# A hybrid GLA, RWKV-7 and SSD layer with 32 experts on one core: the opening's loads and the place of eight small products are moved

## The chip, the cores and the metric

The kernel runs on one core of a Trainium2 chip. The time is the device time of one execution in microseconds (us), from which the median of several runs is taken. The matrix engine is called PE (TensorE), the vector engine DVE (VectorE), the activation engine ACT (ScalarE), the general engine POOL (GpSimd), and SP is the engine that issues the DMAs (SyncE).

## The reference

One layer over 256 latent tokens (x) and 256 context tokens (ctx), model width 1024:

```
mod_l = split(silu(c) @ w_ada + b_ada, 6); mod_c = the same for c_ctx
hl = modulate(rmsnorm(x, norm1_g), mod_l[0], mod_l[1])      # h * (1 + scale) + shift
hc = modulate(rmsnorm(ctx, norm1_g), mod_c[0], mod_c[1])
u  = h @ w_in      -> q, k, v, og, gates (GLA) | RWKV-7 | z, x, B, C, dt (SSD)
x, B, C of the SSD group: silu(depthwise convolution of width 4 over the tokens + bias)
GLA:  o_t = sum_s q_t k_s exp(cum_t - cum_s) v_s, both directions
RWKV-7 and SSD: chunked scans in both directions, the context first
xl = x + mod_l[2] * (concat(gla, rwkv, ssd) @ w_out)
hl = modulate(rmsnorm(xl, norm2_g), mod_l[3], mod_l[4])
moe: router, top 4 of 32 experts; act = glu * sigmoid(1.702 glu) * (lin + 1) ; y += gate * (act @ w_down + b)
out = rmsnorm(xl + mod_l[5] * y, final_norm_g)
```

All weights of the 32 experts are read once: 12 MB each.

## The kernel before, in words

The program is written out by hand for each engine; the order in the code is the order in which an engine runs. Engines meet at semaphores. Results of PE lie in banks of PSUM; a table (`round_table`) gives every result a name and a pair of banks, and a result may only be written (`R.claim`) when the one before it in the same pair has been read out (`R.drained`). B, xs0 and z0 use pair 0 in turn; C, xs1 and z1 pair 1; the nine levels l0 to l8 pair 2; gs, gc, Bt and gS pair 3.

**The opening.** Eight slices k of 128 features each need `ada[k]` (the modulation weights, 1 MB) and `opened[k]` (576 KB: the transposed tokens and a part of the weights); `tokens` (4 DMAs of 512 KB) serve only the root mean squares. ACT squares the four token tiles and takes the root, DVE the reciprocal, and PE spreads the reciprocals over the partitions (`roots_spread`, 4 products). A row of modulation (`modulation_row`, 32 products), its copy by ACT and two products (`modulation_columns`) give the scales of a slice; DVE and ACT scale the slice, and PE projects it. In between PE does `stay_busy(n)`: n products of the identity that nobody reads, in the numbers WARM. A product of this kernel is in fp32 and stands as two matmuls in the trace, so stay_busy(26) is x52.

**The levels.** GLA's causal products are built in nine levels. POOL writes the arguments of a level (4 instructions, L788 to L791), ACT takes their exponent (`level_exp`, L945), DVE multiplies them with keys and queries (`level_keys(i)`, L1424, which feeds level i+1), PE multiplies (`level(i, 0)` and `level(i, 1)`, 4 small products each), and DVE takes the result out (`level_out(i)`; L1249, L1251, L1254). Level i may start when `level_out(i-1)` has read the pair of banks. POOL's arguments of level i+2 wait for `level_keys(i)`. Between the levels PE projects; a half projection (early, late) is 4 products of 128x512.

**Convolutions.** A convolution starts on ACT (`conv_start`, L899) with the centre tap, goes on with `convolve` on DVE (L1345, 12 instructions for 512 tokens), and ends with silu on ACT (`conv_end`). `convolve` also frees the banks of its projection. `multiplied(n)` (L1292, L1290) are DVE's products of later modulation weights, one for each `ada` DMA, between the rest; it frees the slot for a later DMA.

**The experts.** SP loads 12 MB for each of 32 experts into a ring of slots that PE frees.

Of the kernel before, what the change touches and what calls it, by code (L numbers as in the profile page):

```python
# [169 lines left out]
WARM = (10, 4, 26, 7)  # L170
# [21 lines left out]
def round_table():  # L192
    t = []
    for m in range(KD):
        t += [(f"row{m}", 4, 1), (f"col{m}", 2, 1 if m == KD - 1 else 0)]
        if m == 0:
            t.append(("roots", 2, 0))
    t += [("ll", 3, 2), ("gq", 1, 1), ("gv", 0, 1), ("dtp", 4, 1), ("gz", 2, 1), ("og", 1, 1), ("dt", 3, 1), ("gk", 2, 1), ("B", 0, 1),
          ("gvt", 2, 1), ("gs", 3, 1), ("gc", 3, 1)]
    t += [("C", 1, 1), ("ms1", 4, 1), ("mt1", 4, 1), ("xs0", 0, 1), ("xs1", 1, 1)]  # L200
    t += [(f"l{i}", 2, 1) for i in range(9)]
    t += [("z0", 0, 1), ("z1", 1, 1), ("Bt", 3, 1), ("gS", 3, 1), ("rk", 1, 1), ("sc", 0, 1), ("cc", 3, 1), ("xst0", 2, 1), ("go", 3, 1), ("xst1", 2, 1)]
    t += [("ms2", 4, 1), ("mt2", 4, 1), ("rz0", 1, 1), ("cs", 3, 1), ("rz1", 1, 1), ("rr", 0, 1), ("gn", 3, 1), ("st", 1, 1), ("sg", 1, 1), ("rkn", 1, 1)]
# [71 lines left out]
def hybrid_block(nc, a):  # L275

    with ExitStack() as ctx:
# [202 lines left out]
        ident_in = sem("ident_in")  # L480
# [10 lines left out]
        silu_c, root_ready, rms_ready, mod_ready = named("silu_c root_ready rms_ready mod_ready")  # L491
# [18 lines left out]
        f_sq, out_ready, out_done, half_up, bias_up = named("f_sq out_ready out_done half_up bias_up")  # L510
# [76 lines left out]
        for s, width, kind, n in loads:  # L587
            base[s] += 1
            place[kind, n] = (s, base[s])
            if kind == "opened":  # L590
                continue
            before[kind, n] = sorted({h for h in holder[s:s + width] if h})
            given[s] += 1
            free_at[kind, n] = (s, given[s])
            for q in range(s, s + width):
                holder[q] = (s, given[s])
# [33 lines left out]
        def _(sp):  # L630
# [11 lines left out]
            sp.dma_start(Cb(C_ID), a["consts"][:, 0:P]).then_inc(ident_in, 16)  # L642
            for k in range(KD):
                if k == 1:
                    for i in range(4):
                        sp.dma_start(xtok[:, i, :], a["tokens"][i]).then_inc(x_in[i], 16)
                load_ada(k)
                sp.dma_start(opened[:, k, :], a["opened"][k]).then_inc(slot_full[ADA_SLOTS[k]], 16)
                if k in (3, 6):
                    load_ada(8 + k // 4)  # L650
# [204 lines left out]
        def _(act):  # L855
# [16 lines left out]
            def row_copied(m):  # L872

                R.arrived(act, f"row{m}")
                R.drained(f"row{m}", act.copy(modrow[:, 64 * m:64 * m + 64], pair(f"row{m}", 512)[:, 64 * m:64 * m + 64]))

            row_copied(0)
# [6 lines left out]

            for k in range(KD):
                act.wait_ge(mod_ready, k + 1)
                if k == 0:
                    act.wait_ge(rms_ready, 2)
# [63 lines left out]

            level_exp(0)
            level_exp(1)
            conv_start("B")
# [302 lines left out]
        def _(dve):  # L1258
# [18 lines left out]

            def multiplied(n):

                sl, nth = place["ada", n]  # L1280
                if n == 16:
                    R.arrived(dve, "ms1")
                dve.wait_ge(slot_full[sl], 16 * nth)
                by_row = csil[:, n % 8, 0:1]
                flat = mod_products.rearrange("p m c -> p (m c)")
                if n % 8:
                    last, count = free_at["ada", n - 1]
                    dve.wait_ge(slot_free[last], count)
# [14 lines left out]
            for k in range(KD):  # L1303
                s, nth = place["opened", k]
                dve.wait_ge(slot_full[s], 16 * nth)
                if k:
                    step(dve.tensor_tensor(raw[:, k, :], raw[:, k, :], pair("roots")[:, 0:NT], ALU.mult))
# [10 lines left out]
                if k == 0:  # L1318
                    dve.wait_ge(root_ready, 1)
                    dve.reciprocal(small[:, 12:16], small[:, 8:12]).then_inc(rms_ready, 1)  # L1320
                    R.arrived(dve, "roots")
                    dve.tensor_tensor(raw[:, 0, :], raw[:, 0, :], pair("roots")[:, 0:NT], ALU.mult).then_inc(rms_ready, 1)
                    dve.wait_ge(rms_ready, 2)
# [103 lines left out]
            R.emptied(dve, "gq")  # L1427
            level_keys(0)
            level_keys(1)
            level_out(dve, 0)  # L1430
            convolve(0, "B")
# [417 lines left out]
            def activate(n, up_done, by_halves=False):  # L1849
# [3 lines left out]
                for half in range(2):  # L1853
# [4 lines left out]
                    if by_halves:  # L1858
                        of_half = lambda x: PS[:, half, 256 * x:256 * x + 256].rearrange("p (q k) -> p q k", k=2)
                        if half == 0:  # L1860
                            dve.wait_ge(half_up, 1)
                        else:
                            up_done()
# [104 lines left out]
        def _(pe):  # L1968
# [48 lines left out]
            def roots_spread():  # L2017

                R.claim(pe, "roots")
                pe.wait_ge(rms_ready, 1)  # L2020
# [108 lines left out]

            modulation_row(0)  # L2130
# [3 lines left out]
            roots_spread()  # L2134
            stay_busy(WARM[3])
# [45 lines left out]
            project_in("C", 1)  # L2181
            level(1, 0)
            project_in("xs0", 0, early)
            level(1, 1)
            project_in("xs0", 0, late)
            level(2, 0)
            project_in("xs0", 1, early)
            level(2, 1)
            project_in("xs0", 1, late)
            level(3, 0)  # L2190
            project_in("xs1", 0, early)
            level(3, 1)
            project_in("xs1", 0, late)
            modulation_sums(1)
            level(4, 0)
            project_in("xs1", 1, early)
            level(4, 1)
            project_in("xs1", 1, late)
            sums_by_feature(1)
            def running_sums(q):  # L2200
# [619 lines left out]
            def up_by_halves(n, at, hidden, between):  # L2820
# [13 lines left out]
                for j in range(4):  # L2834
                    r, used = at(j)
                    pe.wait_ge(ring_full[r], used * 16 + 16)
                    for k, hf in ((2 * j, 0), (2 * j + 1, 0), (2 * j, 1), (2 * j + 1, 1)) if j == 3 else ((2 * j, 0), (2 * j, 1), (2 * j + 1, 0), (2 * j + 1, 1)):
                        ins = part(k, hf)
                        if (k, hf) == (7, 0):
                            ins.then_inc(half_up, 1)  # L2840
# [3 lines left out]
                    if 1 <= j < 3:  # L2844
                        x = j - 1
                        pe.wait_ge(te_ready, n + 1)
                        if x:
                            pe.wait_ge(bias_up, 1)
# [4 lines left out]
                        if x == 0:  # L2853
                            ins.then_inc(bias_up, 1)
# [224 lines left out]
```

## Time and profile before

| what | value |
|---|---|
| median of 3 runs | 1322.54 us (1314.92, 1322.54, 1323.43) |
| the profiled execution | 1317.88 us |
| its span, first to last instruction | 1316.1 us |
| PE busy | 1246.7 us, 95% |
| DVE, ACT, POOL busy | 401.6, 261.2, 50.4 us |
| DMA, mean over the span | 347 GB/s |

The profile is of one execution, 1.8 us of which lie outside the span. Times in the views count from the span's start. Up to some 200 us the engines share the work of the projections; from there to 370 us run the scans, and from 410 us the experts.

### The profile page before, as it was taken

How to read it: one execution, taken by the hardware profiler on the slowest of the kernel's cores; microseconds unless marked ns; L12 is line 12 of the kernel's file. 1: busy time of each engine (PE TensorE's matmuls, PEld its weight loads, DVE VectorE, ACT ScalarE, POOL GpSimd, SP SyncE). 2: the span in 40 equal slices, each digit the busy share in tenths (PEclk: the TensorE clock that was granted, in tenths of full speed). 3: DMA queues.
4: the chain of work that ended last, by engine and by line, in shares of the span. 5: the costliest groups of instructions: out<-in, count | busy, mean ns of one | idle time of the engine just before them, and what ended most of it. 6: DMA issues, size and time to landing. Idle time of an engine off the chain costs nothing.

```text
span 1316.1 us, 22353 instructions
## 1 busy us (share of the span) xinstructions
PE 1246.7 (95%) x9546; PEld 589.9 (45%) x9546; DVE 401.6 (31%) x906; ACT 261.2 (20%) x601; POOL 50.4 (4%) x89
## 2 busy tenths in 40 slices
PE   8999999889899999999999999999999999999997
PEld 6464656678874333333333333333333333333333
DVE  1457766654442211121111221211221111121112
ACT  3142218543332110111100110100111010011001
POOL 0022100311100000000000000000000000000000
PEclk9999999999999999999999999999999999999999
DMA  9953520243479999999999999999999999999994
GB/s 377 397 193 128 220 108 1 90 144 96 125 279 384 425 426 427 428 429 429 426 429 429 430 427 427 429 430 429 427 428 427 428 428 427 428 427 428 426 427 200
DMA packets 41407, 456.13 MB, mean 347 GB/s; under 512 B 4624, under 2 KB 4880, under 8 KB 12912
## 3 DMA queue, kind: packets, MB, share of 16 engines
q1 hardware_dynamic: 41328, 454.96, 83.1%
q8 instruction: 64, 1.05, 0.3%
q14 instruction: 15, 0.12, 0.0%
HBM read 453.89 MB, written 1.05 MB: 346 GB/s over the span
## 4 chain that ended last, share of the span: by engine, by line
PE 84%; DVE 6%; DMA 5%; issue 2%; ACT 1%; POOL 0%; SPq 0%; DVEq 0%
PE PS L1972 80%; DMA arena<-in_moe_w_gu 3%; DMA arena<-in_moe_b_down 2%; PE PS L2869 2%; DVE arena L1865 1%; DVE arena L1868 1%; DVE arena L1871 1%; PE PS L2860 1%; DVE arena L1345 1%; PE PS L1986 1%; DVE arena L1864 1%; DMA arena<-in_opened 1%; PE PS L2464 0%; POOL arena L790 0%; DVE arena L1965 0%
## 5 line engine op out<-in xcount | busy, mean ns | idle before, releaser
L1972 PE MATMUL PS<-arena 128*64 128x512 f32 (+12 forms) x9174 | 1200.3, 402 | 26.0 <-issue 10.4
L1972 PEld LDWEIGHTS PS<-arena 64*64 64x64 f32 (+6 forms) x9174 | 549.4, 144 | 627.4 <-issue 563.6
L1864 DVE TENSOR_SCALAR arena<-PS 128x256 f32<-128x256 f32 x64 | 38.6, 604 | 505.8 <-PE PS L1972 505.8
L1178 ACT ACTIVATE arena<-arena 128x256 f32<-128x256 f32 x64 | 26.7, 417 | 477.2 <-DVE arena L1864 477.2
L1893 DVE TENSOR_TENSOR arena<-PS,arena 128x512 f32<-128x512 f32 x32 | 22.1, 692 | 214.5 <-PE PS L1972 214.5
L1188 ACT COPY arena<-PS 128x256 f32<-128x256 f32 x32 | 11.9, 373 | 281.0 <-PE PS L2860 281.0
L2869 PE MATMUL PS<-arena 128*128 128x128 f32 x128 | 26.3, 287 | 32.6 <-DVE arena L1871 32.6
L1169 ACT ACTIVATE arena<-PS,arena 128x128 f32<-128x128 f32 x128 | 48.2, 457 | 35.7 <-PE PS L1972 35.7
L2869 PEld LDWEIGHTS PS<-arena 128*128 128x128 f32 x128 | 14.3, 141 | 59.9 <-DVE arena L1871 43.0
L1630 DVE COPY arena<-PS 128x384 f32<-128x384 f32 (+2 forms) x48 | 23.4, 490 | 54.1 <-PE PS L1972 53.7
L1865 DVE TENSOR_SCALAR arena<-PS 128x256 f32<-128x256 f32 x64 | 39.1, 612 | 0.0
L1345 DVE SCALAR_TENSOR_TENSOR arena<-PS,arena 128x255 f32<-128x255 f32 (+5 forms) x68 | 32.6, 481 | 20.2 <-ACT arena L980 14.0
L1292 DVE SCALAR_TENSOR_TENSOR arena<-arena 128x2048 f32<-128x2048 f32 x14 | 33.1, 2363 | 7.0 <-DMA arena<-in_ada 6.9
L1091 ACT COPY arena<-PS 128x384 f32<-128x384 f32 (+2 forms) x48 | 20.5, 427 | 58.7 <-PE PS L1972 58.6
L1868 DVE SCALAR_TENSOR_TENSOR arena<-arena 128x256 f32<-128x256 f32 x64 | 27.2, 425 | 3.9
L1871 DVE TENSOR_TENSOR arena<-arena 128x256 f32<-128x256 f32 x64 | 27.2, 426 | 2.3
L1183 ACT COPY arena<-PS 128x256 f32<-128x256 f32 x64 | 23.7, 370 | 4.3 <-PE PS L2869 4.3
L1840 DVE TENSOR_SCALAR arena<-arena 128x128 f32<-128x128 f32 x64 | 19.1, 342 | 0.0
L1986 PE MATMUL PS<-arena 128*128 128x128 f32 x94 | 14.5, 323 | 3.3 <-DMA arena<-in_consts 3.3
L2860 PEld LDWEIGHTS PS<-arena 128*128 128x128 f32 x64 | 6.5, 141 | 24.3 <-issue 24.3
L1827 DVE TENSOR_SCALAR arena<-arena 128x64 f32<-128x64 f32 x64 | 15.7, 308 | 2.0 <-PE PS L1972 1.9
L1986 PEld LDWEIGHTS PS<-arena 128*128 128x128 f32 x94 | 13.7, 233 | 3.5 <-DMA arena<-in_consts 3.3
(263 smaller groups left out, 395.0 us busy)
## 6 DMA issues: line engine op xcount, KB each, us to landing
arena<-in_moe_w_gu SPq DMA_DIRECT2D x124, 2048.0 KB, 22.5
arena<-in_moe_w_down SPq DMA_DIRECT2D x63, 2048.0 KB, 24.3
arena<-in_ada SPq DMA_DIRECT2D x24, 1024.0 KB, 7.4
arena<-in_w_in SPq DMA_DIRECT2D x4, 2048.0 KB, 9.6
arena<-in_moe_w_gu SPq DMA_DIRECT2D x32, 256.0 KB, 3.0
arena<-in_opened SPq DMA_DIRECT2D x8, 576.0 KB, 19.0
arena<-in_tokens SPq DMA_DIRECT2D x4, 512.0 KB, 8.5
arena<-in_w_out SPq DMA_DIRECT2D x2, 1024.0 KB, 5.8
```

The costliest lines, as they stand in the source:

```text
L1169: ins = act.activation(hg[:, buffer, k, :], PS[:, bank, P * j:P * j + P], ACT.Identity, bias=scales[:, 1, k:k + 1], scale=scales[:, 0, k:k ...
L1178: act.activation(sgm[:, 256 * half:256 * half + 256], glu[:, 256 * half:256 * half + 256], ACT.Sigmoid, scale=ALPHA).then_inc(sig_ready, 1)
L1183: act.copy(actT[:, 2 * half:2 * half + 2].rearrange("p a b c -> p (a b c)"), src).then_inc(actT_ready, 1)
L1292: ins = dve.scalar_tensor_tensor(out=flat, in0=slots[sl], scalar=by_row, in1=flat, op0=ALU.mult, op1=ALU.add)
L1345: ins = dve.scalar_tensor_tensor(out=d_, in0=s_, scalar=wgt, in1=d_, op0=ALU.mult, op1=ALU.add)
L1864: dve.tensor_scalar(by_rest(glu), of_half(0), LIMIT, None, ALU.min).then_inc(glu_ready, 1)
L1865: dve.tensor_scalar(by_rest(lin), of_half(1), LIMIT, -LIMIT, ALU.min, ALU.max).then_inc(moe_vec, 1)
L1868: dve.scalar_tensor_tensor(out=lin[:, cols], in0=lin[:, cols], scalar=1.0, in1=glu[:, cols], op0=ALU.add, op1=ALU.mult).then_inc(moe_vec, 1)
L1871: dve.tensor_tensor(act_[:, cols], lin[:, cols], sgm[:, cols], ALU.mult).then_inc(act_ready, 1)
L1972: ins = pe.matmul(out, lhsT, rhs, start=start, stop=stop, skip_group_check=skip)
L1986: pe.matmul(PS[:, 0, 0:P], ident, ident, start=True, stop=True)
L2869: ins = pe.transpose(dst[:, c * P:c * P + P], act_[:, (2 * half + c) * P:(2 * half + c + 1) * P], ident)
```

## The change

SP issues the four token DMAs ahead of `ada[0]` and `opened[0]`. `opened[0]` has a semaphore of its own. ACT takes the squares and the root ahead of copying the first modulation row; DVE's reciprocal stands ahead of the loop over the slices; PE's `roots_spread` stands ahead of the first row. WARM becomes (30, 3, 6): 30 filling products, then the roots, the row, 3, the columns, 6, and the loop. Before it was 10, the row, 4, the columns, 26, the roots, 7.

In the middle ACT starts B's convolution ahead of the exponents of levels 0 and 1, and DVE convolves B ahead of `level_keys(0)`; `level_out(0)` stands ahead of `level_keys(1)`. Every half of levels 1 to 4 stands one half projection later on PE. In the experts two semaphores are made one (`last_up`), in the last expert alone; its waits come to the same.

```diff
-WARM = (10, 4, 26, 7)
+WARM = (30, 3, 6)
...
 def round_table():
-    t = []
+    t = [("roots", 2, 0)]
     for m in range(KD):
         t += [(f"row{m}", 4, 1), (f"col{m}", 2, 1 if m == KD - 1 else 0)]
-        if m == 0:
-            t.append(("roots", 2, 0))
...
             sp.dma_start(Cb(C_ID), a["consts"][:, 0:P]).then_inc(ident_in, 16)
+            for i in range(4):
+                sp.dma_start(xtok[:, i, :], a["tokens"][i]).then_inc(x_in[i], 16)
             for k in range(KD):
-                if k == 1:
-                    for i in range(4):
-                        sp.dma_start(xtok[:, i, :], a["tokens"][i]).then_inc(x_in[i], 16)
                 load_ada(k)
-                sp.dma_start(opened[:, k, :], a["opened"][k]).then_inc(slot_full[ADA_SLOTS[k]], 16)
+                sp.dma_start(opened[:, k, :], a["opened"][k]).then_inc(slot_full[ADA_SLOTS[k]] if k else opened_in, 16)
...
             act.activation(small[:, 60:61], small[:, 59:60], ACT.Sqrt)
-            row_copied(0)
             for i in range(4):
...
             act.activation(small[:, 8:12], small[:, 0:4], ACT.Sqrt, scale=1.0 / D, bias=small[:, 59:60]).then_inc(root_ready, 1)
+            row_copied(0)
...
+            conv_start("B")
             level_exp(0)
             level_exp(1)
-            conv_start("B")
             level_exp(2)
...
+            dve.wait_ge(root_ready, 1)
+            dve.reciprocal(small[:, 12:16], small[:, 8:12]).then_inc(inverse_ready, 1)
...
             R.emptied(dve, "gq")
+            convolve(0, "B")
             level_keys(0)
+            level_out(dve, 0)
             level_keys(1)
-            level_out(dve, 0)
-            convolve(0, "B")
             multiplied(14)
...
+            roots_spread()
             modulation_row(0)
             stay_busy(WARM[1])
             modulation_columns(0)
             stay_busy(WARM[2])
-            roots_spread()
-            stay_busy(WARM[3])
...
             project_in("C", 1)
+            project_in("xs0", 0, early)
             level(1, 0)
-            project_in("xs0", 0, early)
+            project_in("xs0", 0, late)
             level(1, 1)
-            project_in("xs0", 0, late)
+            project_in("xs0", 1, early)
             level(2, 0)
-            project_in("xs0", 1, early)
+            project_in("xs0", 1, late)
             level(2, 1)
-            project_in("xs0", 1, late)
+            project_in("xs1", 0, early)
             level(3, 0)
-            project_in("xs1", 0, early)
-            level(3, 1)
             project_in("xs1", 0, late)
             modulation_sums(1)
+            level(3, 1)
+            project_in("xs1", 1, early)
             level(4, 0)
-            project_in("xs1", 1, early)
-            level(4, 1)
             project_in("xs1", 1, late)
             sums_by_feature(1)
+            level(4, 1)
```

After this `level(5, 0)` comes next on PE in both kernels, then `project_in("z0", 0)`, the transposes of B, `level(5, 1)`, `project_in("z0", 1)` and `level(6, 0)`.

PE's start before: 10 filling products, the row (32x64), 4, the columns (64x4), 26, the roots (128x128 x4), 7, and the first projection.

```order
L1986 MATMUL PS<-arena 128x128 x10
L1972 MATMUL PS<-arena 32x64 x32
L1986 MATMUL PS<-arena 128x128 x4
L1972 MATMUL PS<-arena 64x4 x2
L1986 MATMUL PS<-arena 128x128 x26
L1972 MATMUL PS<-arena 128x128 x4
L1986 MATMUL PS<-arena 128x128 x7
L1972 MATMUL PS<-arena 128x256
```

PE's start in the changed kernel, where lines stand 4 lower.

```order
L1982 MATMUL PS<-arena 128x128 x30
L1968 MATMUL PS<-arena 128x128 x4
L1968 MATMUL PS<-arena 32x64 x32
L1982 MATMUL PS<-arena 128x128 x3
L1968 MATMUL PS<-arena 64x4 x2
L1982 MATMUL PS<-arena 128x128 x6
L1968 MATMUL PS<-arena 128x256
```

The roots moved ahead of the row, and 9 filling products stand behind the row in place of 37.

PE before, from the second half of the projection of xs1 to the transposes of B (L2333): a half projection is 128x512 x4, a level's half 128x128 x4 of L1972, and L2040 is `sums_by_feature(1)`.

```order
L1972 MATMUL PS<-arena 128x512 x4
L1972 MATMUL PS<-arena 128x128 x4
L1972 MATMUL PS<-arena 128x512 x4
L2040 MATMUL PS<-arena 128x128 x4
L1972 MATMUL PS<-arena 128x128 x4
L1972 MATMUL PS<-arena 128x256 x8
L2333 MATMUL PS<-arena 128x128 x4
```

The same place in the changed kernel.

```order
L1968 MATMUL PS<-arena 128x512 x4
L1968 MATMUL PS<-arena 128x128 x4
L1968 MATMUL PS<-arena 128x512 x4
L2036 MATMUL PS<-arena 128x128 x4
L1968 MATMUL PS<-arena 128x128 x8
L1968 MATMUL PS<-arena 128x256 x8
L2328 MATMUL PS<-arena 128x128 x4
```

`level(4, 1)` now stands directly ahead of `level(5, 0)`, as one run of 8.

## Rows read from the trace of the kernel before

**Rows 1.** The page: busy time, and DMA in 40 slices of the span

```profile
PE 1246.7 (95%) x9546; PEld 589.9 (45%) x9546; DVE 401.6 (31%) x906; ACT 261.2 (20%) x601; POOL 50.4 (4%) x89
DMA  9953520243479999999999999999999999999994
```

**Rows 2.** Waits of SP's queue: line, waited for, us in total, times, longest

```profile
SPq L668 <- PE PS L1972: 797.7, 180, 20.2
```

**Rows 3.** A window of the experts: length, busy times, clock, DMA share, GB/s

```profile
440.00:540.00 100.00, 96.94 (x482) 35.68 (x478) 21.34 (x55) 12.70 (x35) 0.00 (x0) 1.00 1.00 427
```

**Rows 4.** The chain that ended last, 0 to 30 us: start, us, what

```profile
2.11 6.74 DMA arena<-in_opened
...
8.98 1.94 PE PS L1972 x64
10.92 2.01 PE PS L1986 x8
...
13.16 6.00 PE PS L1986 x52
19.16 0.89 PE PS L1972 x8
20.06 1.56 PE PS L1986 x14
21.62 8.63 PE PS L1972 x147
```

**Rows 5.** Timeline, 0 to 22 us: start, us, engine, what [idle before, releaser]

```profile
3.33 4.64 PE L1986 MATMUL PS<-arena 128*128 128x128 f32 x20 [3.33 <-DMA arena<-in_consts]
...
11.08 1.06 ACT L880 ACTIVATE arena<-arena 128x1024 f32<-128x1024 f32 x1
...
15.38 0.30 ACT L883 ACTIVATE arena<-arena 128x4 f32<-128x4 f32 x1
15.71 0.18 DVE L1320 RECIPROCAL arena<-arena 128x4 f32<-128x4 f32 x1 [1.97 <-ACT arena L883]
```

**Rows 6.** The token DMAs: from issue to landing; and a window of 5 us

```profile
DMA to landing us min/median/max: 7.5/8.5/9.5
...
5.00:10.00 5.00, 3.98 (x54) 3.72 (x57) 0.00 (x0) 0.72 (x2) 0.00 (x0) 1.00 1.00 405
```

**Rows 7.** A window of PE behind its pause at 102.7 us: length, PE busy, clock, DMA share, GB/s

```profile
105.50:108.52 3.02, 3.02 (x4) 0.50 0.00 0
```

**Rows 8.** Timeline of B: its last half projection, ACT's start, DVE's convolution, xs0

```profile
90.28 4.02 PE L1972 MATMUL PS<-arena 32*128 32x128 f32 x12
...
97.26 1.43 ACT L899 ACTIVATE arena<-PS,arena 128x512 f32<-128x512 f32 x2
99.20 6.16 DVE L1345 SCALAR_TENSOR_TENSOR arena<-PS,arena 128x254 f32<-128x254 f32 x12
105.50 1.19 PE L1972 MATMUL PS<-arena 128*128 128x512 f32 x1 [2.81 <-DVE arena L1345]
```

**Rows 9.** DVE's timeline from `level_out(4)` to `level_out(5)` and behind

```profile
138.00 1.35 DVE L1254 COPY_PREDICATED arena<-arena,PS 128x512 f32<-128x512 int32 x2 [3.42 <-PE PS L1972]
...
139.84 2.35 DVE L1292 SCALAR_TENSOR_TENSOR arena<-arena 128x2048 f32<-128x2048 f32 x1
...
143.16 6.17 DVE L1345 SCALAR_TENSOR_TENSOR arena<-PS,arena 128x254 f32<-128x254 f32 x12 [0.89 <-DVE arena L1298]
149.24 1.36 DVE L1254 COPY_PREDICATED arena<-arena,PS 128x512 f32<-128x512 int32 x2
```

**Rows 10.** Windows: C's end to level 5, level 5 to level 6

```profile
101.98:141.95 39.97, 37.16 (x142) 16.99 (x141) 27.92 (x42) 9.31 (x13) 9.71 (x13) 0.96 0.34 132
141.95:150.97 9.02, 9.02 (x53) 7.46 (x52) 7.74 (x17) 6.14 (x8) 1.70 (x4) 1.00 0.85 323
```

**Rows 11.** POOL's timeline: two instructions of a level's arguments

```profile
91.21 0.40 POOL L789 TENSOR_TENSOR arena<-arena 128x128 f32<-128x128 f32 x1
91.69 2.33 POOL L790 TENSOR_TENSOR arena<-arena 128x128 f32<-128x128 f32 x1
```

More of the change, by code:

```diff
@@ L479, in hybrid_block @@
         named = lambda names: [sem(n) for n in names.split()]
-        ident_in = sem("ident_in")
+        ident_in, opened_in = sem("ident_in"), sem("opened_in")
         consts_in, params_in, mats_in, xT_in = named("consts_in params_in mats_in xT_in")
@@ L490, in hybrid_block @@
         pool_step, kk_norm, shift_init = named("pool_step kk_norm shift_init")
-        silu_c, root_ready, rms_ready, mod_ready = named("silu_c root_ready rms_ready mod_ready")
+        silu_c, root_ready, inverse_ready, mod_ready = named("silu_c root_ready inverse_ready mod_ready")
         conv_init, conv_silu = named("conv_init conv_silu")
@@ L509, in hybrid_block @@
         actT_done, actT_ready, te_ready, extra_pos = named("actT_done actT_ready te_ready extra_pos")
-        f_sq, out_ready, out_done, half_up, bias_up = named("f_sq out_ready out_done half_up bias_up")
+        f_sq, out_ready, out_done, last_up = named("f_sq out_ready out_done last_up")
         def pair(name, n=1024):
@@ L587, in hybrid_block @@
         for s, width, kind, n in loads:
-            base[s] += 1
+            base[s] += (kind, n) != ("opened", 0)
             place[kind, n] = (s, base[s])
@@ L871, in _ @@
             act.activation(small[:, 60:61], small[:, 59:60], ACT.Sqrt)
-            def row_copied(m):
-                R.arrived(act, f"row{m}")
-                R.drained(f"row{m}", act.copy(modrow[:, 64 * m:64 * m + 64], pair(f"row{m}", 512)[:, 64 * m:64 * m + 64]))
-            row_copied(0)
             for i in range(4):
@@ L883, in _, with row_copied @@
             act.activation(small[:, 8:12], small[:, 0:4], ACT.Sqrt, scale=1.0 / D, bias=small[:, 59:60]).then_inc(root_ready, 1)
+            def row_copied(m):
+                R.arrived(act, f"row{m}")
+                R.drained(f"row{m}", act.copy(modrow[:, 64 * m:64 * m + 64], pair(f"row{m}", 512)[:, 64 * m:64 * m + 64]))
+            row_copied(0)
             for k in range(KD):
                 act.wait_ge(mod_ready, k + 1)
-                if k == 0:
-                    act.wait_ge(rms_ready, 2)
                 act.activation(hT[:, k, L:NT], raw[:, k, L:NT], ACT.Identity, bias=mod[:, k, 0:1], scale=A1[:, k, 0:1]).then_inc(h_by_act, 1)
@@ L1304, in _ @@
                 s, nth = place["opened", k]
-                dve.wait_ge(slot_full[s], 16 * nth)
-                if k:
-                    step(dve.tensor_tensor(raw[:, k, :], raw[:, k, :], pair("roots")[:, 0:NT], ALU.mult))
+                if k == 0:
+                    dve.wait_ge(opened_in, 16)
+                else:
+                    dve.wait_ge(slot_full[s], 16 * nth)
+                if k == 0:
+                    R.arrived(dve, "roots")
+                step(dve.tensor_tensor(raw[:, k, :], raw[:, k, :], pair("roots")[:, 0:NT], ALU.mult))
                 R.arrived(dve, f"col{k}")
@@ L1317, in _ @@
                 dve.tensor_scalar(A1[:, k, :], mod[:, 8 + k, :], 1.0, pc[:, 64 + k:65 + k], ALU.add, ALU.mult).then_inc(mod_ready, 1)
[L1318 to L1323, printed above, removed]
                 dve.wait_ge(mod_ready, k + 1)
@@ L1860, in activate @@
                         if half == 0:
-                            dve.wait_ge(half_up, 1)
+                            dve.wait_ge(last_up, 2)
                         else:
@@ L2019, in roots_spread @@
                 R.claim(pe, "roots")
-                pe.wait_ge(rms_ready, 1)
+                pe.wait_ge(inverse_ready, 1)
                 for t in range(4):
@@ L2839, in up_by_halves @@
                         if (k, hf) == (7, 0):
-                            ins.then_inc(half_up, 1)
+                            ins.then_inc(last_up, 1)
                     ins.then_inc(ring_free[r], 1)
@@ L2847, in up_by_halves @@
                         if x:
-                            pe.wait_ge(bias_up, 1)
+                            pe.wait_ge(last_up, 1)
                         for hf in range(2):
@@ L2853, in up_by_halves @@
                         if x == 0:
-                            ins.then_inc(bias_up, 1)
+                            ins.then_inc(last_up, 1)
             def select_back(n):
```

## The prediction, made before the changed kernel ran

> **What bounds the kernel now.** I read the page first: PE is busy for 95% of the span, and the DMA slices stand at 9 from the opening's two on, then fall to between 0 and 5, and stay at 9 from slice 14 to the last but one [rows 1]. In a window of the experts the DMA engines are busy all the time at 427 GB/s while PE is busy 96.9 of 100 us [rows 3], and SP's queue waited 797.7 us for slots that PE frees [rows 2]. So from 410 us on the load stream and PE hold one another at one pace that this change does not touch. What the change can win is a shift: everything ahead of the experts is a chain in which PE's progress frees slots and starts transfers, so a microsecond won at 20 or at 150 us starts the stream a microsecond sooner and stands at the end, if nothing between gives it back. The last expert's merged semaphore has the same two waits and costs nothing. The work is therefore to follow PE's start [rows 4 to 6] and the stretch from C's projection to level 6 [rows 7 to 10].
>
> **The opening, before.** PE's first useful work, the row, waits for `opened[0]`, which lands at 2.11 + 6.74 = 8.85 us. The four squares on ACT end in a root at 15.68 and a reciprocal at 15.89 us [rows 5], but PE is then in 52 filling matmuls until 19.16; only behind them come the roots (0.89) and 14 more (1.56), and the first projection stands at 21.62 [rows 4]. From there the eight slices run back to back on PE. So 3.3 us of the start are filling that outlasts what it fills.
>
> **The opening, after.** Loads: 2.1 MB of tokens go ahead of 1.64 MB of `ada[0]` and `opened[0]`. At the 405 GB/s of [rows 6] these are 5.2 and 4.05 us. The last token then lands at 8.85 - 4.05 + 5.2 = 10.0 us, and `opened[0]` at 8.85 + 5.2 = 14.0. Behind the last token stand one square (1.06), the root (0.30), the reciprocal (0.18) and their gaps, 1.8 us as from 14.1 to 15.89 before [rows 5]: the inverse is there at 11.8.
>
> Filling: 30 products are 60 matmuls. The first 20 took 4.64 us, 232 ns each, and 8 behind the row 2.01 us, 251 ns each, while 52 later took 6.00 us, 115 ns each [rows 4, 5]. By these durations PE ran at 1.2 GHz until about 12.9 us and at 2.4 behind that, though the column of the granted clock says 1.00 there. Where the clock rises in the changed kernel no row shows. Later in the trace it rose after 3.0 us of work [rows 7]; in the opening it had not risen after the first 4.64 us, and rose 4 us into the second stretch. If it rises at time R, the 60 matmuls end at R + (60 - (R - 3.33)/0.232) x 0.115: R = 8.0 gives 12.6, R = 9.5 gives 13.3, R = 12.9 gives 15.1. I take 13.3, since the work is now without a pause from 3.33, and keep both ends. The roots (0.89) end at 14.2, just behind `opened[0]`; so neither load nor reciprocal is late, and the filling bounds the start. Then the row, about 1.35 us at the full clock (1.94 at the lower one), 6 filling matmuls of 115 ns (0.7), the columns (0.25) and 12 more (1.4): the first projection at 14.2 + 3.7 = 17.9 us. The other way to it is shorter: columns at 16.5, then DVE's two small steps and ACT's 0.6 us scaling, 17.8. **Against 21.62 that is -3.7 us**, between -4.0 (R = 8.0, where `opened[0]` is last) and -1.9 (R = 12.9).
>
> What that uncovers: the slices behind need `opened[1]` at about 19.4; the bytes ahead of it are the same in both kernels, and only their order differs, so it lands when it did. `ada[8]`, which SP holds back until the row has freed its slot, is issued some 4 us later (the row ends at 15.5 and not at 10.9), with everything behind it in SP's queue; that is hidden as long as the transfers already issued (slices 0 to 3 and the tokens, 8.7 MB, 21 us at 405 GB/s) run on. I cost it at nothing.
>
> **The middle, before.** PE ends C and level 1's first half at 102.69, and waits 2.81 us for the end of B's convolution, which holds the banks that xs0 wants [rows 8]. Then it runs for 3.02 us at half the clock [rows 7], which is work of 1.5 us: the pause costs 4.3 us in all.
>
> **The middle, after, in the times of before.** B is complete on PE at 90.28 + 4.02 = 94.30. ACT starts the convolution there, not behind two exponents at 97.26, and needs 1.43 us; DVE convolves from 95.8 and is done after 6.16 us, at 102.0 [rows 8]. PE wants xs0 at 102.05, as `level(1, 0)` moved behind it. The wait goes but for 0.1 us, and with it the fall of the clock. `level_keys(0)`, `level_out(0)` and `level_keys(1)` follow to 104.4; level 1 is wanted at 105.6, level 2 at 114, so their new place is covered by a half projection of 3.6 us each.
>
> **Where it is given back.** The levels stand later on PE. Up to level 4 the order holds: between `level(i, 1)` and `level(i+1, 0)` lies a half projection, longer than the 1.35 us of `level_out` [rows 9]. But `level(4, 1)` now stands directly ahead of `level(5, 0)`, and both use pair 2. The stretch from C to level 5 is 39.97 us with 2.81 of wait [rows 10]; without the wait and without the 1.5 us of clock it is 35.7, so `level(4, 1)` ends at 137.7 (137.9 before, though the projections behind it are done 4.3 us sooner). PE then waits 1.35 us for `level_out(4)`. DVE's chain goes on as before: `level_out(4)` and the keys to 139.84, the product of 2.26, the modulation, and the convolution of xs1, which before waited 0.89 us for ACT's start and now does not; 6.1 us of convolution, 1.25 us of `level_out(5)`: read out at 150.5 - 0.9 - 0.1 = 149.5 [rows 9]. `level(6, 0)` needs that. PE itself is there at 137.7 + 1.35 + 9.0 = 148.1 [rows 10] and waits 1.4 us. Before, it began level 6 at 150.97. **The middle wins 1.5 us, not 4.3**: 2.8 us come back as two waits of 1.4. Behind level 6 the same instructions stand in the same order, with DVE's chain and PE's less than 2 us apart, so I let the 1.5 stand. Bounds: 0, if the execution compared with had no fall of the clock (PE would have been 1.5 us earlier at level 6 and the changed kernel no earlier), and -4.3, if the two waits are not there. PE's pauses of 1.4 us are half of the one that let the clock fall; if it falls at the second, 1.5 us go.
>
> **The sum.** -3.7 - 1.5 = -5.2 us. The profiled execution gives 1317.88 - 5.2 = 1312.7, the median of the three 1322.54 - 5.2 = 1317.3. The four executions shown have a mean of 1319.7; I start between, and say 1315.0. A measurement of this kernel can tell about 1%, 13 us, from no change; the forecast is well inside.
>
> **A rule of the skill against the change.** One of POOL's instructions took 2.33 us while DVE was in a product of `multiplied`; its neighbour took 0.40 [rows 11]. Now POOL's arguments of levels 2 and 3 start when `level_keys(0)` and `level_keys(1)` are done, at 102.6 and 104.4, and `multiplied(14)` follows on DVE at 104.4 for 2.3 us. The last of the arguments of level 2 (4 x 0.48 us from 102.6) ends at 104.5: if it is caught, the exponent and behind it C's start on ACT come 2 us late, and `level_out(1)` at 113.9 in place of 112. PE wants the banks at 114.1. The Trainium skill, "SBUF — State Buffer", section "Who interferes with whom", says that a vector instruction with two inputs in SBUF contends with a GpSimd instruction that reads SBUF, and that the one issued first locks the other out; by that rule the trace's 2.33 us is such a lock. It is a rival with a price below.
>
> **The rivals.** (1) Nothing is given back: had `level_out(4)` and DVE's chain slack, the sum is -3.7 - 4.3 = -8.0, 1312. Against it speaks one pair of banks for l4 and l5. 12%. (2) The middle wins nothing, because the clock usually does not fall after 2.81 us, or because it falls again at the new waits: -3.7, 1316.5. The granted clock fell here within that pause. 13%. (3) POOL is locked out and level 2 comes up to 1.5 us late, which goes through to level 4 and eats the middle's gain: -3.7, 1316.5 as well. 6%. (4) The opening wins little: the tokens land as late as before, because the 16 DMA engines serve them beside `ada[0]`; the inverse at 15.9, the roots at 16.8, the projection at 20.5, -1.1; with the middle -2.6, 1317.5. 8%. (5) **Slower**: the clock does not rise while the long filling runs. 60 matmuls of 232 ns end at 17.2, the roots take 1.8 (19.0), the row 1.94, the filling 1.4 and 2.8, the columns 0.3: 25.5 in place of 21.62, +3.9; a second fall at the new waits takes the middle's gain; +3.9 and 1324. It decides from a rise at 16.5 us on, where the filling ends 3.7 us later than I say. For it speaks that the first 4.64 us did not raise the clock. 6%. The forecast keeps 55%.
>
> **The range.** 1306 to 1324: from the lowest execution shown less 9, over all the cases but the slower one, to its edge; what the executions of one kernel differ by (8.5 us among three) is most of it. Faster by over 1% 3%, within 1% 94%, slower by over 1% 3%.
>
> **What would show it.** The first projection on PE at about 17.9 us and not 21.62; the long filling ends at about 13.3, with the roots directly behind; no wait of PE for L1341 at xs0; and two new waits of PE of about 1.4 us, for `level_out(4)` ahead of level 5 and for `level_out(5)` ahead of level 6, with the granted clock at 1.00 between 100 and 110 us. If PE stands idle anywhere ahead of 60 us for a DMA, my cost of nothing for SP's later issues was wrong.

## The result and the profile after

The changed kernel has a median of 1311.39 us (1308.07 to 1316.23, 20 runs) against 1318.05 us (1314.9 to 1324.43, 20 runs): a ratio of 0.995, with an interval from 0.9938 to 0.9963. That is 4.9 to 8.2 us less, 6.6 by the medians, and well under the 1% that I had set as the bound of no change. The interval leaves out 1, so the gain is clear of the noise though it is small. The forecast was 5.2 us less, and 1315.0 us in 1306 to 1324. Of the 3.6 us between 1315.0 and the measured median 2.1 are the start: the forecast took the kernel before at 1320.2 us, and twenty runs have it at 1318.05.

The opening first, as the chain that ended last in the changed kernel (start, us, what). These rows stand against [rows 4].

```profile
3.12 9.77 PE PS L1982 x60
12.89 1.93 PE PS L1968 x72
...
17.43 2.32 PE PS L1968 x68
```

The x60 are the 30 filling products, the x72 the roots and the row, run together without a pause. The filling ends at 12.9 us (forecast 13.3) and the first projection stands at 17.43 (forecast 17.9, before 21.62). 60 matmuls in 9.77 us are 163 ns each, a mix of 232 and 115. PE's matmuls start twice as densely from about 9 us on, so the clock rose there, though the granted clock reads 1.00 on both sides. The timeline of ACT and DVE in the same stretch (start, us, engine, what, idle before it) stands against [rows 5]. It shows that the reciprocal was ready at 11.30 us, 1.6 us before PE looked for it.

```profile
9.61 1.06 ACT L871 ACTIVATE arena<-arena 128x1024 f32<-128x1024 f32 x1
...
11.12 0.18 DVE L1274 RECIPROCAL arena<-arena 128x4 f32<-128x4 f32 x1 [8.01 <-ACT arena L874]
```

The middle is read best on PE's own timeline from xs0 to the head sums, against [rows 8, 10].

```profile
87.47 45.21 PE L1968 MATMUL PS<-arena 128*128 128x512 f32 x174
132.52 0.60 PE L2036 MATMUL PS<-arena 128*128 128x128 f32 x4
133.05 0.71 PE L1968 MATMUL PS<-arena 32*128 32x128 f32 x8
135.31 4.37 PE L1968 MATMUL PS<-arena 32*128 32x128 f32 x24 [1.54 <-DVE arena L1249]
...
145.70 15.51 PE L1968 MATMUL PS<-arena 32*128 32x128 f32 x80 [1.30 <-DVE arena L1249]
161.97 6.22 PE L1968 MATMUL PS<-arena 128*128 128x8 f32 x34 [0.76 <-DVE arena L1491]
```

One line now spans 87 to 132 us: the pause of 2.81 us is gone. In its place stand the two forecast ones, 1.54 us ahead of level 5 and 1.30 ahead of level 6, both released by `level_out` (now L1249). The third, 0.76 us, was there before. DVE's timeline shows where the second wait comes from; it stands against [rows 9].

```profile
133.81 1.35 DVE L1249 COPY_PREDICATED arena<-arena,PS 128x512 f32<-128x512 int32 x2 [5.86 <-PE PS L1968]
135.06 0.68 DVE L1420 TENSOR_TENSOR arena<-arena 128x512 f32<-128x512 f32 x1
135.65 2.34 DVE L1290 SCALAR_TENSOR_TENSOR arena<-arena 128x2048 f32<-128x2048 f32 x1
...
138.12 6.17 DVE L1341 SCALAR_TENSOR_TENSOR arena<-PS,arena 128x254 f32<-128x254 f32 x12
144.21 1.35 DVE L1249 COPY_PREDICATED arena<-arena,PS 128x512 f32<-128x512 int32 x2
```

From 133.81 on DVE is busy without a pause: level 4 out, keys, product, convolution, level 5 out follow one another, after 5.86 us in which DVE waited for PE to come to level 4. Level 6 begins 5.27 us sooner than before (150.97), the head sums 5.26 sooner (before 167.23). Behind that the profiled execution, with 1316.23 us the slowest of the 20, gives back more than half: it is 1.65 us under the profiled execution of the kernel before (1317.88). The last two experiments look at this.

### The profile page after: what moved, and what is told of

Read it like the earlier page. It is cut to its first block, busy times and chain, and to the rows that moved or that the text cites. A ratio compares the mean times of both kernels' runs of the same rounds, so it can differ in the third digit from the quotient of the medians.

```text
span 1314.3 us, 22318 instructions
## 1 busy us (share of the span) xinstructions
PE 1247.0 (95%) x9530; PEld 591.0 (45%) x9530; DVE 402.2 (31%) x906; ACT 261.5 (20%) x601; POOL 52.2 (4%) x89
## 4 chain that ended last, share of the span: by engine, by line
PE 82%; DMA 7%; DVE 7%; issue 2%; ACT 1%; SPq 0%; DVEq 0%
PE PS L1968 78%; DMA arena<-in_moe_w_gu 5%; DMA arena<-in_moe_b_down 2%; PE PS L2864 2%; DVE arena L1861 1%; DVE arena L1341 1%; DVE arena L1864 1%; DVE arena L1867 1%; PE PS L1982 1%; PE PS L2855 1%; DVE arena L1860 1%; PE PS L2459 0%; DVE arena L1290 0%; ACT arena L894 0%; DVE arena L1249 0%
## 5 line engine op out<-in xcount | busy, mean ns | idle before, releaser
L2864 PEld LDWEIGHTS PS<-arena 128*128 128x128 f32 x128 | 14.3, 142 | 59.9 <-DVE arena L1867 43.0
L2855 PEld LDWEIGHTS PS<-arena 128*128 128x128 f32 x64 | 6.5, 141 | 24.3 <-issue 24.3
L1982 PE MATMUL PS<-arena 128*128 128x128 f32 x78 | 12.3, 330 | 3.1 <-DMA arena<-in_consts 3.1
L785 POOL TENSOR_TENSOR arena<-arena 128x128 f32<-128x128 f32 x8 | 10.3, 1289 | 114.3 <-ACT arena L933 85.6
```

Source lines behind the costliest of these rows:

```text
L1982: pe.matmul(PS[:, 0, 0:P], ident, ident, start=True, stop=True)
L2864: ins = pe.transpose(dst[:, c * P:c * P + P], act_[:, (2 * half + c) * P:(2 * half + c + 1) * P], ident)
```

## The experiments

Totals of one kernel differ by 5 to 13 us from run to run, so most readings are taken from PE's timeline: the first projection, level 6, and what lies between them. Where level 6 has no wait ahead of it, it stands inside a longer group: in the second run of the kernel before, the 24 products of level 5 begin at 144.97 and take 4.3 us, so that level 6 begins at 149.27. Each experiment has one profiled execution. The chain has the first projection about 0.1 us later than the timeline; differences are taken within one view. Medians and ratios stand beside them.

**The opening alone.** The kernel before with all edits but those of the middle (ACT's and DVE's order around B, and the levels on PE).

> The kernel before with the opening's part of the change alone (loads, roots, fillings), the middle as before. If the two parts are independent, the first projection stands at 17.4 us as in the changed kernel, level 6 begins at 150.97 - 4.2 = 146.8 with the wait of 2.8 us for B's convolution and the clock's fall still there, and the time is 4.2 us under the kernel before (ratio 0.9968). Rival: the earlier start only lengthens a later wait, as for a load in the stretch from 60 to 100 us; then level 6 stands within 1 us of 150.97.

The first projection stands at 17.5 us. PE's timeline around xs0 has the old pause, and level 6 begins at 147.0.

```profile
94.74 3.83 PE L1968 MATMUL PS<-arena 128*128 128x256 f32 x22
101.39 7.05 PE L1968 MATMUL PS<-arena 128*128 128x512 f32 x18 [2.81 <-DVE arena L1341]
```

Median 1313.45 us, ratio 0.9964 (0.9948 to 0.9981). Level 6 stands 3.9 us sooner for 4.1 us at the first projection, so the opening's gain goes through to level 6, and no load between 60 and 100 us takes it back.

**The middle alone.**

```diff
             R.emptied(dve, "gq")
+            convolve(0, "B")
             level_keys(0)
+            level_out(dve, 0)
             level_keys(1)
-            level_out(dve, 0)
-            convolve(0, "B")
```

with the same edits on ACT and PE as in the change, and the opening as before.

> The kernel before with the middle's part alone (B's convolution first, levels half a projection later). The two waits of about 1.4 us at levels 5 and 6 appear as in the changed kernel, the wait of 2.8 us goes; level 6 begins 1.1 to 1.5 us earlier, at 149.5 to 149.9, and the time falls by as much (ratio 0.999). Rival: all 4.3 us are won in the middle and the changed kernel lost 3 us through its opening; then level 6 stands at 146.7.

PE's timeline has both waits of the changed kernel.

```profile
136.52 0.71 PE L1972 MATMUL PS<-arena 32*128 32x128 f32 x8
138.78 4.37 PE L1972 MATMUL PS<-arena 32*128 32x128 f32 x24 [1.55 <-DVE arena L1254]
...
149.17 11.02 PE L1972 MATMUL PS<-arena 32*128 32x128 f32 x63 [1.29 <-DVE arena L1254]
```

Level 6 stands 1.8 us sooner, of which 0.6 are this execution's own start (20.99 against 21.62). Median 1317.7 us, ratio 0.9998 (0.9985 to 1.0011): the 1.2 us that are left of 4.3 are too little for the total to show. The two halves alone add up to -5.0 us by their ratios.

**Level 4 back beside the projection.**

```diff
             level(4, 0)
-            project_in("xs1", 1, late)
-            sums_by_feature(1)
+            project_in("xs1", 1, range(4, 6))
             level(4, 1)
+            project_in("xs1", 1, range(6, 8))
+            sums_by_feature(1)
```

> The changed kernel with the second half of level 4 back inside the last half projection of xs1 (two products, the level's half, two products), so that its reading out by DVE lies beside the rest of that projection and the sums. My theory: both new waits go, since DVE's chain (level 4 out, keys, product, convolution of xs1, level 5 out) starts 2.4 us earlier and the convolution then follows ACT's start; level 6 begins at 145.70 - 2.4 = 143.3 or a little earlier, and the time falls by 2.4 to 2.8 us against the changed kernel (ratio to before near 0.993). Rival: DVE is full between the two levels, so that only the wait at level 5 goes and the one at level 6 grows by as much; then level 6 stands at 145.7 and nothing is won.

The wait at level 5 is gone. The one at level 6 is still there with 0.56 us, where I had expected both to go.

```profile
133.58 4.36 PE L1968 MATMUL PS<-arena 32*128 32x128 f32 x24
...
138.31 4.37 PE L1968 MATMUL PS<-arena 32*128 32x128 f32 x24
143.23 7.15 PE L1968 MATMUL PS<-arena 32*128 32x128 f32 x41 [0.56 <-DVE arena L1249]
```

DVE takes level 4 out from 131.34 us on, 2.47 sooner than in the changed kernel (133.81), and level 6 begins 2.47 us sooner too, at 143.23 (0.2 of it is the start, 17.21 against 17.43). The rival is out: DVE's chain shifts as a whole with the time at which PE gives it level 4. Its length has not changed, and that is the 0.56 us. Median 1308.98 us, ratio 0.9936 (0.9915 to 0.9957).

**Fewer fillings alone.** The kernel before with one line changed.

```diff
-WARM = (10, 4, 26, 7)
+WARM = (10, 4, 12, 3)
```

> The kernel before with one edit: 12 and 3 filling products in place of 26 and 7 behind the columns. The loads and the roots keep their place. If the filling alone held back the start, the roots follow the reciprocal at 15.9 us, the tokens' scaling and the first projection stand at 18.4 to 18.7 us in place of 21.62, and the time falls by 3 us (ratio 0.9977): most of the opening's gain then needs no other order of loads. Rival: the clock of PE falls without the filling, and the eight slices start at half the clock; then the first projection stands later than 19.5 us or the slices end no earlier than before.

The chain shows the reciprocal, the roots, the scaling of the tokens, ACT's share and the first projection directly one behind another.

```profile
14.99 0.19 DVE arena L1320
...
15.22 1.17 PE PS L1972 x8
...
16.42 0.70 DVE arena L1322
...
17.20 0.61 ACT arena L889
...
17.86 7.24 PE PS L1972 x83
```

17.86 us: 3.8 us under the first profile of the kernel before by this one line, better than I expected (18.4 to 18.7). Part of that is this execution. Its clock rose within the row, which took 1.26 us on PE's timeline and not 1.94, so ACT began the squares at 9.88 and waited for the last token, which was there at 13.5. In the first profile of the kernel before the row and its copy held ACT until 11.08 [rows 5], the four squares ran without a pause behind it, and the last began at 14.21. Against the execution of the kernel before whose clock rose as early (19.71, below) the line wins 1.9 us. The clock did not fall in PE's two short pauses here (1.34 and 0.80 us): the 8 us from the first projection on hold 146 matmuls, and 147 in the changed kernel. The change's own opening, with its new order of loads and roots, stands at 17.43. Median 1311.76 us, ratio 0.9952 (0.9935 to 0.9969), which can't be told from the changed kernel's 0.995, nor from the 0.9964 of the opening alone. In this execution the granted clock was 0.50 (1.2 GHz) for 6.8 us, from 101 to 107.8, after the pause that began at 99 us. That is twice as long as in the first profile, and level 6 stood at 148.8; the fall of the clock has no fixed price.

**The tokens behind.** The changed kernel with the four token DMAs behind the first slice's loads, as before.

> The changed kernel with the order of the loads put back alone: the tokens behind the first slice's two loads. The opening then waits for the reciprocal: the last token lands at 13.5 to 13.9 us, the reciprocal is there at 15.0 to 15.9, and behind it stand roots, row, fillings and columns, 3.7 us as before, and up to 2 us more if the clock falls in PE's pause of 2 to 3 us. First projection at 19.6 to 21.6 us, against 17.3 with the tokens first: the order of the loads is worth 2.3 us or more once the roots stand ahead of the row. Rival: the loads are of no weight, and the projection stands within 0.5 us of 17.3.

PE's timeline: the filling ends at 12.3, PE waits 3.2 us, and behind that all is slow.

```profile
3.15 9.15 PE L1983 MATMUL PS<-arena 128*128 128x128 f32 x60 [3.15 <-DMA arena<-in_consts]
15.50 3.91 PE L1969 MATMUL PS<-arena 128*128 128x128 f32 x72 [3.20 <-DVE arena L1275]
...
22.76 1.46 PE L1969 MATMUL PS<-arena 128*128 128x256 f32 x4
```

22.8 us, past the upper end of what I expected and 1.2 later than the kernel before: roots and row take 3.91 us in place of 1.93, at a granted clock of 0.50. By the chain the first projection stands 5.5 us behind the changed kernel's (22.92 against 17.43): 2.6 of them are the later start of the roots, 2.9 the clock. So the two moves are tied. With the roots ahead of the row the tokens must come first; without either move the short filling alone does nearly as well. Median 1316.22 us, ratio 0.9992 (0.9973 to 1.0011).

**The short filling.** The changed kernel with WARM = (10, 3, 6).

> The changed kernel with 10 filling products in place of 30 at the start. PE then pauses from about 8 us to the reciprocal at 11.1. If the long filling was what bounded the start (it ended at 12.9 in the changed kernel), the roots start at 11.2 and the row waits for its load at 13.5, which wins at most 0.3 us; if the filling is needed for the clock, the roots, the row and the next fillings run at 1.2 GHz (1.8, 1.9, 1.4 and 2.8 us) and the first projection stands at about 19 to 20 us, 2 to 3 later. I expect the second.

```profile
3.08 4.63 PE L1982 MATMUL PS<-arena 128*128 128x128 f32 x20 [3.08 <-DMA arena<-in_consts]
11.41 3.91 PE L1968 MATMUL PS<-arena 128*128 128x128 f32 x72 [3.69 <-DVE arena L1274]
15.25 1.23 PE L1982 MATMUL PS<-arena 128*128 128x128 f32 x6
```

The first projection stands at 18.1 us, 0.8 later than in the changed kernel and not 2 to 3. Roots and row do take twice as long (3.91 us again; the granted clock reads 1.00 there, as at every start), but they begin 1.5 us sooner, and the clock is up while the next fillings run. The 20 more products are worth 0.8 us, not much more than two executions of the changed kernel differ by here (17.43 and 16.84). Median 1313.91 us, ratio 0.9975 (0.9956 to 0.9993).

**Filling the pause.** The kernel before with 12 filling products ahead of xs0.

```diff
             level(1, 0)
+            for _ in range(12):
+                pe.matmul(PS[:, 7, 0:P], ident, ident, start=True, stop=True)
             project_in("xs0", 0, early)
```

> The kernel before with 12 more filling products (24 matmuls of 0.11 us, 2.6 us) in PE's pause ahead of xs0, in a bank that nobody holds. The wait for the convolution stays filled, the clock should not fall. My theory (the pause costs 2.8 us of waiting and 1.5 of clock): xs0 still starts at 105.5 us, and level 6 begins at 149.5 in place of 150.97, without a wait for level 5's reading out. Rival: the fall of the clock cost nothing that DVE's chain would not have cost, and level 6 stays at 151.0.

```profile
102.23 2.94 PE L2184 MATMUL PS<-arena 128*128 128x128 f32 x24
105.13 7.09 PE L1972 MATMUL PS<-arena 128*128 128x512 f32 x22
```

xs0 starts at 105.13 at a granted clock of 1.00: 22 matmuls in 7.09 us, where with the opening alone 18 took 7.05. Level 6 begins at 149.12, 1.85 us sooner, of which 0.4 are the start of this execution. The clock's part of the pause was 1.5 us, and reached level 6 whole, because DVE had that much slack in the old order. So 12 products that nobody reads win as much at level 6 as the middle's whole rearrangement. Median 1315.17 us, ratio 0.9986 (0.9969 to 1.0003), which the total alone does not tell from nothing.

**Level 4 back and shorter fillings together.** The changed kernel with the edit of level 4 above and WARM = (25, 0, 7).

> The changed kernel with level 4's second half back between xs1's products, and with 25, 0 and 7 filling products in place of 30, 3 and 6. The filling then ends 0.6 us sooner, the row is bound by its load at 13.5, the columns by ACT's copy, 0.35 us sooner than behind 3 fillings: first projection at 16.6 to 16.9 us in place of 17.05 to 17.27. Level 6 begins at 142.7 to 143.0, the ratio to before is 0.993 or a little under, 2.5 us under the changed kernel. Rival: the shorter filling lets the clock rise later, and what the opening wins is lost in the row and the slices.

```profile
4.07 8.23 PE L1982 MATMUL PS<-arena 128*128 128x128 f32 x50 [4.07 <-DMA arena<-in_consts]
12.14 2.09 PE L1968 MATMUL PS<-arena 128*128 128x128 f32 x72
...
16.44 9.05 PE L1968 MATMUL PS<-arena 128*128 128x256 f32 x148
```

The first projection stands at 16.44 us, level 6 at 142.45, both 0.2 to 0.3 us sooner than I had expected at the least. Median 1306.03 us (1303.38 to 1309.37), ratio 0.9919 (0.9894 to 0.9945): the best version, 11 us under the kernel before as run beside it (1317.31). Against the changed kernel's median, from another batch, it is about 5 us less, where I had expected 2.5; level 6 shows 2.4 to 3.3 of these (144.84 and 145.70 against 142.45), the rest is not explained.

**DVE's product later.** The version just above with `multiplied(17)` moved from behind `level_keys(5)` to behind `level_keys(6)`.

> The version with level 4 back in the last half projection and 25, 0 and 7 filling products, with one more edit: DVE's product that stood between level 4's keys and xs1's convolution (2.3 us) stands behind level 6's keys. If DVE's chain sets level 6, the convolution starts with ACT's start at hand (134.0 us in place of 134.9) and the wait of 0.56 us of PE at level 6 goes; level 6 begins at 141.9 in place of 142.45. The product's slot is then freed 9 us later, and the loads behind it in SP's queue with it. Rival: those later loads (two modulation slices and the weights of rk) make DVE or PE wait between 150 and 175 us, and the head sums, at 158.71 in the version without the edit, come later.

Level 6 did begin without a wait, at 141.98. But the rival was right. The moved product freed its slot at 144.44, SP issued the next `ada` load at 144.46, and DVE waited for it ahead of level 6's reading out, which came at 151.54 in place of 147.51. DVE's timeline and, in the middle line, PE's:

```profile
149.27 2.35 DVE L1290 SCALAR_TENSOR_TENSOR arena<-arena 128x2048 f32<-128x2048 f32 x1 [2.38 <-DMA arena<-in_ada]
...
153.03 12.19 PE L1968 MATMUL PS<-arena 32*128 32x128 f32 x36 [2.39 <-DVE arena L1249]
158.04 2.35 DVE L1290 SCALAR_TENSOR_TENSOR arena<-arena 128x2048 f32<-128x2048 f32 x1 [4.59 <-DMA arena<-in_ada]
```

The version above waits for `in_ada` too (1.74 and 3.91 us), but where PE does not stand still for it. Here PE waited 2.39 us, and the granted clock was 0.50 from 153 to 163 us. The head sums came at 164.6 in place of 158.7. Median 1314.19 us, ratio 0.9985 (0.9964 to 1.0006): half a microsecond won at one wait cost 8 us against the version above (1306.03), by medians of different batches.

**Both kernels once more.**

> The kernel before once more, unchanged. Its first projection and level 6 should stand within 0.7 us of the first profile (21.5 and 151.0). Open is the stretch of the scans: if the falls of the granted clock there go with the execution and not with the change, this profile may show some between 240 and 370 us, where the first had none, and a stretch from 170 to 370 us longer by half of their length.

> The changed kernel once more, unchanged. First projection at 17.3 and level 6 at 145.7, within 0.7 us. If the falls of the clock between 240 and 370 us (10.2 us of low clock in its first profile) belong to the change, they are there again with about the same length; if they go with the execution, their number and length differ.

The kernel before took 1322.29 us this time, the changed one 1308.98, each in a single execution. The first projection of the kernel before stood at 19.7 us, 1.9 sooner than in its first profile and outside what I expected: the clock rose earlier, so that the row and the 8 matmuls of filling behind it took 1.10 and 1.09 us in place of 1.94 and 2.01 [rows 4]. The chain of this execution:

```profile
8.85 1.10 PE PS L1972 x64
9.95 1.09 PE PS L1986 x8
...
11.25 6.00 PE PS L1986 x52
...
19.71 5.69 PE PS L1972 x78
```

The falls of the clock in the scans go with the execution: the changed kernel had 10.2 us at half the clock there in its first profile, as in these windows (length, busy times, granted clock, DMA share, GB/s), and none in its second. The kernel before had none in its first and about 3.4 us in its second (359 to 363 us). Of all thirteen profiles seven have such a fall between 240 and 370 us, in both orders of the middle.

```profile
268.50:271.80 3.30, 3.30 (x32) 2.97 (x34) 1.00 (x3) 2.88 (x7) 0.00 (x0) 0.50 0.55 156
353.80:360.60 6.80, 5.71 (x113) 5.43 (x108) 1.86 (x6) 1.44 (x3) 0.00 (x0) 0.50 0.35 115
```

The first load of the expert stream was issued at 370.9 and 372.2 us in the two profiles of the kernel before, at 367.1 and 362.4 in those of the changed one. From there to the end of the span it is 945.2 and 948.2 us, and 947.2 and 944.7: the stream itself differs by up to 3.5 us between executions, about as much as one half of the change wins.

## Why the prediction was right

**The opening** (forecast -3.7). The first pair of profiles gives 17.43 - 21.62 = -4.2. Over four executions with each opening the first projection stands at 21.62, 19.71, 20.99 and 21.23 (the kernel before twice, the middle alone, the pause filled) and at 17.43, 16.84, 17.53 and 17.21 (the changed kernel twice, the opening alone, level 4 back): 20.9 against 17.25, -3.6. The steps held one by one: the long filling bounds the start, the reciprocal (11.3 us) and the load are there when PE comes for them. The clock rose at about 9.0 us, where I took 9.5. That -3.7 meets -3.6 so closely is in part luck. The forecast subtracts from 21.62, the latest of the four starts and 0.7 us behind their mean, and puts the new start at 17.9, 0.65 behind its mean, nearly all of it in the end of the filling (12.3 to 13.0 us, forecast 13.3); the two errors cancel. What the forecast left unsaid is that the new order of loads and roots hardly matters here: the fillings alone give 17.86. It also counted from 14.1 us as if the last square had waited for its token, where ACT was still busy with the squares before it; the 1.8 us from there on held all the same (9.61 to 11.30, 1.7).

**The loads issued later at no cost**: right; between the first projection and 60 us PE stands idle once, for 0.31 us and not for a load, and the opening's gain reaches level 6.

**The middle** (forecast -1.5, against the obvious -4.3). From the first projection's start on the timeline to level 6 the old order takes 129.4, 129.6 and 129.7 us (the kernel before twice: 150.97 - 21.53 and 149.27 - 19.63; the opening alone: 147.04 - 17.37), the new one 128.4, 128.3 and 128.2 (the changed kernel: 145.70 - 17.27; the middle alone: 149.17 - 20.91; the changed kernel again: 144.84 - 16.68): -1.3 in the mean. With the fewer fillings, whose clock stayed low for 6.8 us, the old order took 130.9; with it the difference is -1.6. Both waits stand where the forecast put them, with 1.54 and 1.30 us for 1.35 and 1.4, and the version with level 4 back removes 2.3 of these 2.8 us by one edit, which shows that the waits come from the place of level 4, and not only that they are there.

**The rivals.** That nothing is given back (-8.0) is refuted by the two waits; the totals, with 4.9 to 8.2 us, could hardly have told it from the forecast. That the tokens land as late as before is refuted by ACT's squares, the last of which began at 9.61. That the clock's fall is not typical is refuted too: all four executions with the old pause show it (the kernel before twice, the opening alone, the fewer fillings). The slower rival, a clock that stays low through the long filling, did not come. What did cost the whole gain, in the version with the tokens behind, was a wait of PE between filling and roots, with the fall of the clock behind it. POOL's slow instruction came again, as in [rows 11], but in another place than I had priced: its fourth instruction for level 2 took 0.73 us, and the first for level 3 took 2.45 us beside DVE's product (100.46 to 102.94 us). C's start on ACT still came at 101.36, and PE waited for none of it. This is POOL's timeline in the changed kernel.

```profile
100.07 0.73 POOL L788 TENSOR_TENSOR arena<-arena 128x128 f32<-128x128 f32 x1
100.75 2.45 POOL L785 TENSOR_TENSOR arena<-arena 128x128 f32<-128x128 f32 x1
```

The Trainium skill, "SBUF — State Buffer", section "Who interferes with whom", says that the second SBUF input of a DVE instruction comes through the read interface that it shares with GpSimd; the rows agree with it, since POOL's 2.45 us end 0.3 us behind DVE's product, which took 2.48. The rival's mechanism is there and its price is not: the exponent of level 3 was ready at 105.6 us, and DVE's keys for it began at 116.5, 11 us later.

**What stays open.** The milestones add up to -3.6 - 1.3 = -4.9 us, the lower end of the measured 4.9 to 8.2; the medians say 6.6. The rest, if it is one, lies behind 170 us, where single executions differ by several microseconds, in part with the falls of the clock in the scans. Two profiles of each kernel do not show whether the changed kernel has fewer of these on average. That a microsecond won ahead of the scans stands whole at the end is argued from the chain and fits the order of most medians, but it is not shown to better than a few microseconds. The fewer fillings are the plainest case: their median is 6.3 us under the kernel before, and level 6 stood only 2.2 us sooner in their profile, which is of the slowest of their seven runs. One reading of [rows 1] was off and nothing hangs on it: the DMA slices rise to 7 at the twelfth and stand at 9 from the thirteenth on.

## What to carry to other kernels

Where a pause is taken out of the middle of a pipeline, go on to the next place at which the same banks are read out directly between two users: moving work later by half a step made two products of one pair of banks neighbours, and a reading out of 1.35 us that had been covered stood bare. Filling work that keeps the clock up must be cut to what it waits for: 18 products too many cost 1.9 us where the clock had risen early in both executions and 3.8 us against the first profile, more than the new order of loads and roots won on top (17.86 against 17.25 us). Cutting past the point where PE has to wait gave 0.8 us back. And a wait of half a microsecond is not worth moving an instruction that frees a slot for a queue of loads.

## What the runs showed of the hardware

I had not expected that the price of one pause of 2.8 us would vary so: it was followed by 3.4 us at half the clock in the kernel before and by 6.8 us in the run with fewer fillings, with the same length of pause. With 12 products in its place the granted clock stayed at 1.00, in one execution. Nor had I expected that a fall may cost nothing: with the tokens behind, PE ran at half the clock for 3.4 us from 140.9 us on, and level 6 came 128.4 us after the first projection as in the changed kernel, because DVE's chain set it. Of two pauses of 1.5 and 1.3 us, 9 us apart, the first was followed by a fall in one of the five executions that have it (the tokens behind), the second in none of the four that have it.
